# Expert loop of a mixture-of-experts layer: the rows of four experts' first steps gathered in one buffer and shared out to the tokens by six full products

## What is computed

```python
gates = jnp.sum(jax.nn.one_hot(ids, N_EXPERTS) * weights[..., None], axis=1)   # two non-zero per token
hg = jnp.einsum('nd,edf->nef', t, w_gate)
hu = jnp.einsum('nd,edf->nef', t, w_up)
y = jnp.einsum('nef,efd->nd', jax.nn.silu(hg) * hu * gates[:, :, None], w_down)
x = x + gate * y
```

## Time and profile before

| what | value |
|---|---|
| median of 3 runs | 1239.99 us (1237.75 to 1240.44) |
| the profiled execution | 1240.41 us, its span 1238.7 us |
| granted clock of TensorE, mean | 0.953 |
| TensorE, weight loads, VectorE, ScalarE, GpSimd busy | 91%, 52%, 45%, 22%, 14% |
| mean transfer rate | 254 GB/s |

### The profile page before, as it was taken

How to read it: one execution, slowest core, us unless ns; L and a number is a source line. 1 busy time by engine, 2 the same in 40 slices (tenths; PEclk the granted TensorE clock), 3 DMA queues, 4 the chain that set the end, 5 groups by cost and what they waited for, 6 DMA issues and landing times.

```text
span 1238.7 us, 26144 instructions
## 1 busy us (share of the span) xinstructions
PE 1126.9 (91%) x9179; PEld 644.5 (52%) x9180; DVE 563.0 (45%) x1196; ACT 268.8 (22%) x648; POOL 172.8 (14%) x261
## 2 busy tenths in 40 slices
PE   6999979999888999999699999999998798999995
PEld 4644646654654555555456653344556454555553
DVE  1031265643543444444434235777455334444445
ACT  2211235631121222121222222221021211222221
POOL 0152120000121111211000001111011111112110
PEclk9999999999798999999899998998996989999998
DMA  9856899740998999999512211000139899987893
GB/s 361 310 186 225 280 327 327 269 131 4 374 358 337 404 422 423 421 421 391 211 68 83 87 69 68 0 1 0 71 104 361 333 376 374 420 346 286 334 423 159
DMA packets 82734, 314.19 MB, mean 254 GB/s; under 512 B 11160, under 2 KB 12097, under 8 KB 57321
## 3 DMA queue, kind: packets, MB, share of 16 engines
q1 hardware_dynamic: 77658, 300.56, 62.6%
q0 software_dynamic: 1952, 6.90, 1.6%
q10 hardware_dynamic: 3056, 5.77, 1.2%
HBM read 307.82 MB, written 5.39 MB: 253 GB/s over the span
## 4 chain that ended last, share of the span: by engine, by line
PE 83%; DVE 6%; DMA 4%; issue 4%; SPq 2%; ACT 1%; POOL 0%; ACTq 0%; POOLq 0%; DVEq 0%
PE banks L472 80%; DVE arena L1046 4%; DMA arena<-in_ada_b 3%; DMA arena<-token_rows,arena 1%; PE banks L669 1%; SPq L1961 1%; PE banks L764 1%; SPq L1959 1%; PE banks L888 0%; DVE arena L1196 0%; PE banks L615 0%; POOL arena L1849 0%; DVE arena L1206 0%; PE banks L523 0%; DVE banks L1046 0%
## 5 line engine op out<-in xcount | busy, mean ns | idle before, releaser
L472 PE MATMUL banks<-arena 32*128 32x256 f32 (+10 forms) x8752 | 1072.5, 415 | 78.9 <-issue 37.1
L472 PEld LDWEIGHTS banks<-arena 128*32 128x32 f32 (+5 forms) x8752 | 593.2, 153 | 533.3 <-issue 410.2
L1046 DVE TENSOR_TENSOR arena<-banks,arena 128x64 f32<-128x64 f32 (+3 forms) x282 | 113.2, 413 | 69.2 <-PE banks L472 63.4
L1046 DVE TENSOR_TENSOR arena<-arena 128x384 f32<-128x384 f32 (+12 forms) x239 | 138.8, 588 | 4.5
L1314 DVE SCALAR_TENSOR_TENSOR arena<-arena 128x768 f32<-128x768 f32 x81 | 84.4, 1042 | 107.3 <-issue 105.0
L1700 ACT ACTIVATE arena<-banks 128x512 f32<-128x512 f32 x79 | 47.2, 597 | 223.8 <-PE banks L472 222.2
L1856 POOL TENSOR_TENSOR arena<-arena 128x256 f32<-128x256 f32 x81 | 59.4, 733 | 260.3 <-PE banks L472 242.7
L1324 DVE TENSOR_SCALAR arena<-arena 128x64 f32<-128x64 f32 x79 | 15.8, 199 | 162.2 <-ACT arena L1704 162.2
L1882 POOL COPY arena<-arena 128x256 f32 x77 | 30.5, 397 | 155.8 <-PE banks L472 152.2
L1836 POOL TENSOR_SCALAR arena<-arena 128x8 f32<-128x8 f32 (+2 forms) x28 | 6.8, 244 | 315.7 <-ACT arena L1547 227.9
L1414 DVE TENSOR_SCALAR arena<-arena 128x385 f32<-128x385 f32 x24 | 11.6, 481 | 82.4 <-ACT arena L1761 82.4
(11 more groups left out here) (151 smaller groups left out, 446.8 us busy)
## 6 DMA issues: line engine op xcount, KB each, us to landing
arena<-in_moe_w_gate SPq DMA_DIRECT2D x64, 1024.0 KB, 8.2
arena<-in_moe_w_up SPq DMA_DIRECT2D x64, 1024.0 KB, 10.6
arena<-in_moe_w_down SPq DMA_DIRECT2D x64, 1024.0 KB, 10.9
arena<-in_ada_w SPq DMA_DIRECT2D x24, 2048.0 KB
arena<-in_hy_w_in SPq DMA_DIRECT2D x6, 2048.0 KB
arena<-in_attn_w_in SPq DMA_DIRECT2D x3, 2048.0 KB
arena<-mod_rows SPq DMA_DIRECT2D x8, 512.0 KB, 9.2
arena<-in_attn_w_out SPq DMA_DIRECT2D x2, 2048.0 KB
```

The lines of the kernel that those rows point to most:

```text
L472: return pe.matmul(out, lhsT, rhs, start=start, stop=stop, skip_group_check=True)
L1046: return dve.tensor_tensor(o, p, q, op)
```

## The change

Rows of first steps are no longer shared out step by step. GpSimd copies them from ysb in four pieces of 32 partitions into Y4, a buffer of 128 rows (4 experts x 32) by 1024 channels, which exists twice. VectorE builds one `share4` for the four experts of a round, in slot 0 of the next round. TensorE multiplies share4 by Y4 in six full products (128x128 by 512 columns), two in each of the slots 1 to 3 of the next round, around `summed`; the last round's six stand behind the loop. Second steps keep the 12 small products (`shared`), in two halves of six, both ahead of `summed`, with yprev and share of the second step before. The copy to xcur moves from GpSimd to VectorE (`take`), which is now unrolled over four experts, has three value loads per expert, and does the share addition of a second step behind a wait for TensorE's `shared` of that step. TensorE and GpSimd read a parity with one more value load per round. The first copy to xcur stands behind the third XS copy of VectorE. The table, the accumulators' places in PSUM and the semaphores follow.

```diff
+    t[:, 756:760] = M * (np.arange(P)[:, None] // M == np.arange(4))
+    t[:, 760:760 + NE // 4] = np.arange(NE // 4) % 2
...
-            b = place["acc", l * 6 + (q if t < 2 else 4 + q // 2)]
-            c = (t if t < 2 else q % 2) * DE
-            return ps[:, b, c:c + DE] if n == 1 else ps[:, b:b + 2, c:c + DE] if t < 2 else ps[:, b, :].rearrange("p (q c) -> p q c", q=2)
+            b = place["acc", l * 6 + 2 * t + q // 2]
+            c = q % 2 * DE
+            return ps[:, b, c:c + n * DE]
...
-        share, share_last = v(HTO + 2304, NTOK), v(HTO + 2304 + NTOK, NTOK)
+        share, share4 = v(HTO + 2304, NTOK), v(HTO + 2304 + NTOK, NTOK)
+        Y4 = v(HO + D, 2, D)
+        first4_row = v(WORK + 10096, NE // 4)
...
-                acc = [(("acc", l * 6 + i), [("xffn", l * 3 + (1 if i < 4 else 2))], 2 + i) for i in range(6)]
+                acc = [(("acc", l * 6 + i), [("xffn", l * 3 + i // 2)], 2 + i) for i in range(6)]
...
-                def first_half(shares, rows_, start=False):
-                    two = ((2, 0), (2, 2), (0, 1), (0, 3), (0, 0), (0, 2), (1, 1), (1, 3))
-                    share_parts(two, shares, rows_, start).then_inc(s_["moe_half"], 1)
-
-                def second_half(g, shares, rows_, start=False):
-                    pe.wait_ge(s_["moe_half"], g + 1)
-                    return share_parts(((1, 0), (1, 2), (2, 1), (2, 3)), shares, rows_, start).then_inc(s_["moe_shared"], 1)
-
-                def summed(g):
+                def shared(g, start=False):
+                    share_parts(((0, 0), (0, 2), (1, 1), (1, 3), (2, 0), (2, 2)), share, yprev, start).then_inc(s_["moe_sums"], 1)
+                    pe.wait_ge(s_["moe_sums"], g * 2 + 1)
+                    share_parts(((0, 1), (0, 3), (1, 0), (1, 2), (2, 1), (2, 3)), share, yprev, start).then_inc(s_["moe_shared"], 1)
+
+                def four_shared(t, hf, par):
+                    o = share_sum(l, t, 2 * hf, 2)
+                    c = slice(hf * 512, (hf + 1) * 512)
+                    return mm(o, share4[:, t * P:(t + 1) * P], Y4[:, bass.ds(par, 1), c].rearrange("p o n -> p (o n)"), False, False)
+
+                def summed(g, counts):
                     pe.wait_ge(s_["moe_g"], g + 1)
                     pe.wait_ge(s_["moe_y"], g + 1)
                     for c in range(4):
                         last = mm(pt[:, c * M:(c + 1) * M], gsb[:, c // 2, :, c % 2], sel)
-                    last.then_inc(s_["moe_pt"], 1)
-
-                def one_step(g, slot, before):
+                        if c < len(counts):
+                            last.then_inc(s_[counts[c]], 1)
+                    last.then_inc(s_["moe_sums"], 1)
+
+                def first_step(g, slot, r, par):
                     hidden(g, slot)
-                    down_product(g, before)
-                    pe.wait_ge(s_["moe_share"], g + 1)
-                    pe.wait_ge(s_["moe_move"], g + 1)
-                    first_half(share, yprev)
-                    summed(g)
-                    second_half(g, share, yprev)
+                    if slot == 1 and par is not None:
+                        pe.wait_ge(moe_four, 17 * l + r * 2 + 1)
+                        pe.wait_ge(moe_rows, 4 * NE * l + r * 16)
+                    down_product(g, (slot - 1) % 4)
+                    if slot and par is not None:
+                        four_shared(slot - 1, 0, par)
+                    summed(g, ("moe_sums", "moe_shared"))
+                    if slot and par is not None:
+                        last = four_shared(slot - 1, 1, par)
+                        if slot == 3:
+                            last.then_inc(moe_round, 1)
+
+                def extra_step(g, slot):
+                    hidden(g, slot)
+                    down_product(g, slot)
+                    pe.wait_ge(s_["moe_share"], g)
+                    pe.wait_ge(s_["moe_extra"], g)
+                    shared(g)
+                    summed(g, ())
...
+                    par = None if first else pe.value_load(tbi[0:1, bass.ds(r + 95, 1)], min_val=0, max_val=1)
...
-                            first_half(share, ysb, True)
-                            summed(b)
-                            pe.wait_ge(s_["moe_move"], 1)
-                            second_half(0, share, ysb, True)
+                            shared(0, True)
+                            summed(b, ())
                         else:
-                            one_step(b, s, (s - 1) % 4)
+                            first_step(b, s, r, par)
...
-                                one_step(b + j, s, s)
+                                extra_step(b + j, s)
...
-                pe.wait_ge(s_["moe_share"], g + 1)
-                pe.wait_ge(s_["moe_move"], g + 1)
-                first_half(share, yprev)
-                second_half(g, share, yprev)
-                pe.wait_ge(s_["moe_shared"], g + 2)
-                sig("share_last").at(pe, l)
-                pe.wait_ge(s_["moe_y"], g + 1)
-                first_half(share_last, ysb)
-                second_half(g + 1, share_last, ysb)
+                pe.wait_ge(s_["moe_share"], g)
+                pe.wait_ge(s_["moe_extra"], g)
+                shared(g)
+                pe.wait_ge(moe_four, 17 * l + 2 * (NE // 4) + 1)
+                pe.wait_ge(moe_rows, 4 * NE * (l + 1))
+                for t in range(T):
+                    for hf in range(2):
+                        last = four_shared(t, hf, (NE // 4 - 1) % 2)
+                    last.then_inc(moe_round, 1)
...
+                begins = pref[:, 32:64].rearrange("p (r s) -> p s r", s=4)
+                link(dve.tensor_scalar(first4_row, begins[:, 0, :], row_group[:, 0:1], None, ALU.mult))
+                for k in range(1, 4):
+                    link(dve.scalar_tensor_tensor(first4_row, begins[:, k, :], row_group[:, k:k + 1], first4_row, ALU.mult, ALU.add))
...
+                def take(g, first):
+                    first = nc.s_assert_within(first, 0, SLOTS, skip_runtime_bounds_check_because="a step starts at a slot of its expert")
+                    dve.wait_ge(s_["moe_pg"], g + 1)
+                    dve.tensor_copy(xcur, XS[:, :, bass.ds(first, M)]).then_inc(s_["moe_x"], 1)
+
+                def activated(g):
+                    dve.wait_ge(s_["moe_e"], g)
+                    dve.tensor_scalar(e1, ex, 1.0, None, ALU.add).then_inc(s_["moe_dve"], 1)
+                    dve.wait_ge(s_["moe_dve"], g * 4 + 1)
+                    dve.reciprocal(e2, e1).then_inc(s_["moe_dve"], 1)
+                    dve.wait_ge(s_["moe_dve"], g * 4 + 2)
+                    tt(e1, ptv[:, 0], e2, ALU.mult).then_inc(s_["moe_dve"], 1)
+                    dve.wait_ge(s_["moe_dve"], g * 4 + 3)
+                    tt(aT, ptv[:, 1], e1, ALU.mult).then_inc(s_["moe_a"], 1)
+
+                def extra_share(g, r):
+                    c = nc.s_assert_within(g + 1, 0, MAXSTEPS, skip_runtime_bounds_check_because="a step is one of MAXSTEPS")
+                    dve.wait_ge(s_["moe_share"], g)
+                    dve.wait_ge(moe_four, 17 * l + r * 2 + 1)
+                    dve.scalar_tensor_tensor(parts, posr, first_row[:, bass.ds(c, 1)], wr, ALU.is_equal, ALU.mult).then_inc(s_["moe_dve"], 1)
+                    dve.wait_ge(s_["moe_dve"], g * 4 + 4)
+                    dve.wait_ge(s_["moe_shared"], g + 1)
+                    tt(share, parts[:, 0, :], parts[:, 1, :], ALU.add).then_inc(s_["moe_share"], 1)
+
+                def four_share(i, g):
+                    dve.wait_ge(s_["moe_share"], g)
+                    dve.scalar_tensor_tensor(parts, posr, first4_row[:, bass.ds(i, 1)], wr, ALU.is_equal, ALU.mult).then_inc(moe_four, 1)
+                    dve.wait_ge(moe_four, 17 * l + i * 2 + 2)
+                    dve.wait_ge(moe_round, 12 * l + i + 2)
+                    tt(share4, parts[:, 0, :], parts[:, 1, :], ALU.add).then_inc(moe_four, 1)
+
+                def four_experts(r, first):
+                    for s in range(4):
+                        n, b = steps_of(dve, r * 4 + s)
+                        o = dve.value_load(tbi[0:1, bass.ds(r * 4 + s + 2 * NE, 1)], min_val=0, max_val=SLOTS)
+                        if not (first and s == 0):
+                            take(b, o)
+                            activated(b)
+                            dve.sem_inc(s_["moe_dve"], 1)
+                        dve.sem_inc(s_["moe_share"], 1)
+                        if s == 0 and not first:
+                            four_share(r - 1, b)
+                        with dve.If_ne(dve.to_reg(n), 1):
+                            with dve.Fori(1, n) as j:
+                                take(b + j, o + j * M)
+                                activated(b + j)
+                                extra_share(b + j, r)
+
+                dve.sem_inc(s_["moe_dve"], 4)
+                dve.sem_inc(moe_four, 1)
...
+                    if i == 2:
+                        sig("xs_a").at(dve, l * ST)
```

(58 more changed lines are left out.)

56 lines of the change are left out of this document (13 added, 43 removed).

## The result

The changed kernel takes **1291.11 us** (median of 4 runs, 1285.7 to 1296.88), the kernel before 1238.87 beside it (4 runs, 1235.35 to 1240.44). The ratio is 1.040, 95% interval 1.036 to 1.045. It is slower by 52 us; the forecast was 1295.

A forecast was written before the change was run, and what follows sets the result against it. It took TensorE, busy 91% of the span, as the bound, with first steps hanging on its queue's chain. Terms -1.3 + 38.4 + 7.0 + 10.2 + 0.4 = +54.7 us gave 1295 us, range 1254 to 1314.

The forecast's parts named there:

- Second steps: In both expert loops, VectorE's copy, queued behind the share addition and three value loads, delays the next hidden product: +38.4 us.
- Rival A: VectorE's queue goes on past a waiting operation, so value loads finish during the share addition's wait; 1255 us, chance 0.14.
- First steps: Expert loops: shorter TensorE chain behind ysb, -9.3 us, against a third value load in later rounds, +8.0; together -1.3 us.
- I take 0.15 us a first step: Saving per first step from a dozen fewer small instructions between TensorE's wait for ysb and its loads; bounds 0 and 0.37.
- The parity load: Third value load on TensorE ahead of a later round's first hidden product: 0.73 us each, 11 counted, +8.0 us.
- The round end: Sign to look for: a first step that ends a round, 6.41 us before the change, comes near 7.0 us.
- The loops' starts: First copy into xcur waits for VectorE's third XS copy; second hidden product comes 3.5 us later a layer: +7.0 us.
- The clock: TensorE's 2.0 us stalls in second steps lower its clock in 6 of 15, up to 1.7 us each: +10.2 us.
- The end: After each layer's last shared, ysb, four copies and two products take 4.6 us against 4.37; +0.4 us in all.
- Rival B: TensorE's chain behind ysb is shorter, engine time decides; first steps 5.5, about 4.8 in slot 0; 1231 us, chance 0.10.
- Rival C: Each stall lowers the clock (25.5 us), or new code comes late on first passes; 1310 us and up, chance 0.14.

## Why the prediction was right

The number, 1295 for 1291, is right by its main term, and partly by errors that cancelled.

- **Second steps: right, in mechanism and size.** Forecast 38.4 us, measured 37.0. The share addition was put at h + 5.20 and came at h + 5.18; the copy 2.61 later, measured 2.58; the step at 8.2, measured 8.06 (8.10 in the rows shown); the pause at 2.0, measured 1.95 to 2.1. At the round end 8.4 was taken and 8.47 measured. With the loads ahead the stall was gone.
- **Rival A is refuted.** Its second step, 6.2, is what the run with the loads ahead has (6.04). VectorE did not go on to the loads while the addition waited. The prediction says that no row shows a value load; the chain view does (above), and with it the reason. The wait for TensorE's `shared` is an instruction of its own in VectorE's queue, line 1356, ahead of the addition, and the queue stands at it. An operation that carries its own wait holds the queue as well: the activation's first (line 1342) idled for over 1 us 46 times, and each time the queue's next instruction starts 0.01 us (13 to 15 ns) behind its start, never in the idle time. The Trainium skill (Perfetto Trace Analysis, DVE / Act Engine Instruction) has it that a waiting instruction is set aside in a queue and the sequencer is free for the next one. These 46 disagree with it, and so do GpSimd's rows in the prediction; the share addition doesn't test it, since its long wait stands ahead of it.
- **First steps: right sign of each part, the saving mis-sized.** The term "I take 0.15 us a first step" was 0.28 in slots 1 and 2 and 0.49 in slot 0; in slot 0 that is above the bound of 0.37. The bound took TensorE's engine for the next limit; with the products left out too, a step is 5.39 to 5.46, so the queue's chain decides down to there, and the two products add 0.1 to it in slots 1 and 2. The trace shows the saving where the term looked for it: TensorE's queue passed the wait for ysb at 463.75 and came to the two loads at 464.30 before the change, at 446.50 and 446.64 after it, 0.55 us against 0.14. The parity load was put at 0.73 and measured 0.75 (6.69 to 5.94). The term -1.3 should have been -11.5, which lies in its bounds of -15 to +10.
- **The round end** was said to come near 7.0 and came at 6.69: 0.73 for the load, less the same mis-sized saving (6.40 + 0.75 - 0.46).
- **The loops' starts:** 3.5 a layer was forecast up to the second hidden product, 1.3 of it ahead of the first. Measured at full clock are 1.07 for the first copy, and then 1.9 in layer 0 and 1.5 in layer 1 (10.7 and 10.4 us against 8.9 in most variants): 5.6 in both layers instead of 7.0, near the lower bound of 2.5 a layer. The profiled run has 5.0 between the two hidden products, with some 1.7 of clock in it. Left out of the sum altogether were the five new operations in the routing, 1.05 us a layer ahead of the loop.
- **The clock: right mechanism, half its size.** "6 of 15 pauses at 1.7", 10.2 us, stands against a remainder of 24 us in the loops. Filling the pauses gives back some 18. The term was mis-sized in what it counted: it priced pauses of 2 us alone. First steps themselves lost clock: in the kernel before, none of the 57 warm steps has any time at the lower clock, while after the change 14 of the 44 first and 5 of the 13 second ones have. TensorE has less work in each step, and taking more away cost more (1.0801, one second step more included), putting some back in slot 0 gave it back (1.0108 to 1.0032). The range's 25 for this term held it.
- **The end** at +0.4 measured +0.3 (23.4 us from the last hidden product, before 23.1).
- **Not foreseen:** 6 us less between the loops, by the clock.

Put together: 37.0 - 11.5 + 5.0 + 24.2 = 54.7 in the loops, + 2.1 ahead, - 6.0 between, + 0.3 behind = 51.1, the difference of the spans. The clock's 24.2 is what the other terms leave, so this sum closes of itself. The forecast's errors (first steps +10.2, second steps +1.4, starts with all that is ahead of the first loop -0.1, clock -14.0, end +0.1, between the loops +6.0) come to +3.6, its 54.7 against 51.1. That first steps, clock and the stretch between the loops cancel to within 2.2 us is luck.

**Rival B** asked whether first steps hang on the engine. By the products taken out they don't: 5.4 to 5.5 is the chain, not 4.8 in slot 0. **Rival C's** clock loss of 25.5 came in size (24 us), though not from the stalls alone, and without the late code that it named; a pause of that kind appeared only where an experiment made VectorE's code longer.

**What stays open:** why the executions with the parity's load moved have a lower clock than those of the kernel after, when 2.7 us of steps is all that the edit costs; whether the half clock of 95.6 us against 78.5 is the moved load's at all, since the clocks of the two kernels overlap; and which of the idler steps cost how much clock.

## What to carry to other kernels

Before a waiting operation is put on an engine, look at the register loads that stand behind it: if a value is known earlier, load it ahead of the wait (here 2 us in each of 15 steps hung on three loads). Fewer instructions on an engine that waits anyway buy little, and they can cost clock, as on TensorE here: price the clock for each step that gets idler, not only for the pauses that you can see. Where branches are restructured, count the instruction packets in every copy of the loop. And compare the clocks of all executions before two traces are compared: one of them may be the fastest of its kernel and the other the slowest.
